# One expert load of the last step, split by rows into one transfer of 96 and four of 8

## The reference

```
def expert_block(args):
    xb, e = args
    return (jax.nn.silu(xb @ w1[e]) * (xb @ w3[e])) @ w2[e]
...
out = jnp.zeros((N + 1, D), jnp.float32).at[row_tok].add(yr.astype(jnp.float32) * row_w[:, None])
```

## Time and profile before

| | us |
|---|---|
| median of 3 runs (lowest to highest) | 675.09 (674.52 to 675.24) |
| the profiled execution, its own time | 675.29 |
| its span, from the first to the last instruction | 673.5 |
| PE busy in the span | 511.5 (76%) |
| DMA busy, mean of 16 engines, by the first queue | 89.4% |

### The profile page before, as it was taken

The page is one execution under the profiler, slowest core; times in us unless marked ns, Lnnn a source line. Parts: engine busy times, 40 slices in busy tenths (PEclk is TensorE's granted clock), DMA queues, the critical chain, the costliest instruction groups (busy, mean ns, idle before and its releaser), DMA issues.

```text
span 673.5 us, 8778 instructions
## 1 busy us (share of the span) xinstructions
PE 511.5 (76%) x3804; PEld 322.7 (48%) x3804; DVE 204.5 (30%) x378; ACT 145.5 (22%) x252; POOL 14.9 (2%) x31
## 2 busy tenths in 40 slices
PE   8999999999999997967744846774374667348475
PEld 7999998999999742422311411231141123114121
DVE  4899565588857431100000100000010000001002
ACT  5764545354635411000000000000000000000002
POOL 1200010001001000000000000000000000000001
PEclk9999999999999988997857988786797778679788
DMA  8999236908679999999999999999999999999994
GB/s 290 386 325 326 90 126 198 372 4 300 224 279 387 417 366 431 427 427 427 430 424 431 424 431 424 432 423 429 428 427 429 425 430 427 428 426 429 425 410 168
DMA packets 46041, 244.21 MB, mean 363 GB/s; under 512 B 5968, under 2 KB 15664, under 8 KB 34224
## 3 DMA queue, kind: packets, MB, share of 16 engines
q1 hardware_dynamic: 46000, 243.62, 89.4%
HBM read 242.53 MB, written 4.22 MB: 366 GB/s over the span
## 4 chain that ended last, share of the span: by engine, by line
PE 53%; DMA 44%; DVE 1%; ACT 1%; issue 0%; SPq 0%; POOL 0%; POOLq 0%
PE ps L713 16%; DMA slots_late<-in_w 13%; PE ps L1077 11%; DMA slots_own<-in_w 9%; DMA attn_data<-in_w 7%; PE ps L736 7%; PE ps L1082 6%; DMA slot_spare<-in_w 5%; DMA slot_last<-in_w 5%; DMA slot_mixed<-in_w 4%; PE ps L691 1%; DMA slots_own<-in_w_in 1%; PE ps L837 1%; PE ps L866 1%; PE ps L1187 1%; PE ps L951 1%
## 5 line engine op out<-in xcount | busy, mean ns | idle before, releaser
L1077 PE MATMUL ps<-slots_late,x_sb 128*32 128x512 f32 x320 | 88.2, 697 | 36.6 <-DMA slots_late<-in_w 14.7
L1077 PE MATMUL ps<-slot_spare,x_sb 128*32 128x512 f32 x128 | 60.8, 675 | 13.7 <-DMA attn_data<-in_w 13.7
L1077 PE MATMUL ps<-attn_data,x_sb 128*32 128x512 f32 x160 | 61.9, 701 | 10.7 <-DMA slots_own<-in_w 10.7
L1820 DVE TENSOR_TENSOR slot_extra<-ps,slot_extra 128x512 f32<-128x512 f32 x8 | 5.5, 692 | 212.2 <-ACT slot_extra L1443 212.2
L439 DVE TENSOR_TENSOR w_low<-slots_own,w_high 128x2048 fp32r<-128x2048 f32 (+1 forms) x32 | 64.7, 2021 | 16.8 <-ACT w_high L1251 16.5
L1440 ACT ACTIVATE slot_extra<-ps 128x256 f32<-128x256 f32 x8 | 3.1, 384 | 299.7 <-PE ps L1145 299.7
L1077 PE MATMUL ps<-slots_own,x_sb 128*32 128x512 f32 x240 | 56.7, 664 | 8.8 <-DMA slot_last<-in_w 3.6
L1082 PE MATMUL ps<-slots_own,slot_extra 128*32 128x512 f32 x192 | 50.1, 723 | 16.1 <-DMA slots_late<-in_w 8.0
L1082 PE MATMUL ps<-attn_data,slot_extra 128*32 128x512 f32 x112 | 46.4, 749 | 16.4 <-DMA slots_own<-in_w 16.4
L1251 ACT ACTIVATE w_high<-slots_own 128x2048 fp32r<-128x2048 f32 (+1 forms) x32 | 54.3, 1697 | 19.5 <-PE ps L736 10.8
L713 PE MATMUL ps<-h_high,w_high 128*128 128x256 f32 x224 | 55.4, 288 | 0.0
(11 more groups left out here) (262 smaller groups left out, 868.5 us busy)
## 6 DMA issues: line engine op xcount, KB each, us to landing
slots_own<-in_w SPq DMA_DIRECT2D x27, 2048.0 KB, 31.4
slots_late<-in_w SPq DMA_DIRECT2D x23, 2048.0 KB, 35.0
attn_data<-in_w SPq DMA_DIRECT2D x16, 2048.0 KB, 34.3
slot_last<-in_w SPq DMA_DIRECT2D x9, 2048.0 KB, 35.9
slots_own<-in_w_in SPq DMA_DIRECT2D x8, 2048.0 KB, 10.9
slot_spare<-in_w SPq DMA_DIRECT2D x8, 2048.0 KB, 34.7
slot_mixed<-in_w SPq DMA_DIRECT2D x7, 2048.0 KB, 34.7
slots_own<-in_w_out SPq DMA_DIRECT2D x2, 2048.0 KB, 9.7
```

Source lines behind the costliest of these rows:

```text
L1077: return pe.matmul(ps[SLOTS * e:SLOTS * e + SLOTS, 4 + matrix, :], xeT[:, k, SLOTS * e:SLOTS * e + SLOTS], w, start=(k == 0), stop=(k == K ...
L1820: dve.tensor_tensor(act_sb, ps[:, 5, :].rearrange("p (q f) -> p f q", f=FC), silu_sb.rearrange("p (f q) -> p f q", f=FC), ALU.mult).then_i ...
```

## The change

Unit 84 is no longer one transfer of 128 rows. SP issues five: rows 0 to 95 in one, which adds to `slot_in` as before, and then rows 96 to 103, 104 to 111, 112 to 119 and 120 to 127 in four, which add to a new semaphore, `split_rows_in`. PE waits for that semaphore (4 times 16) as well before the last step's first matmul. The transfer of 96 rows is spread over all sixteen DMA engines, each transfer of 8 rows over half of them. Bytes, slots and the order of the loads are the same.

```
+SPLIT_UNIT = (STEPS - 1) * MOE_CHUNKS
+SPLIT_ROWS = [(0, 96)] + [(p0, 8) for p0 in range(96, P, 8)]
...
-        extra_in = sem("extra_in")
+        extra_in, split_rows_in = sem("extra_in"), sem("split_rows_in")
...
+                elif q == SPLIT_UNIT:
+                    matrix, expert = j // SHARE, step * SHARE + j % SHARE
+                    for p0, n in SPLIT_ROWS:
+                        sp.dma_start(ring[s][p0:p0 + n].unsqueeze(1),
+                                     expert_weights[matrix][p0:p0 + n, expert:expert + 1, :]
+                                     ).then_inc(split_rows_in if p0 else slot_in[s], 16)
...
                     pe.wait_ge(slot_in[s], value)
+                    if it * MOE_CHUNKS + j == SPLIT_UNIT:
+                        pe.wait_ge(split_rows_in, 16 * (len(SPLIT_ROWS) - 1))
```

## The result

The changed kernel takes 686.46 us (median of 6 runs, 685.27 to 689.67), the kernel before 675.10 beside it (6 runs, 674.32 to 675.69): a ratio of 1.0175, interval 1.0164 to 1.0187, or 11.4 us more. The forecast was 673.9, its range ended at 679.9. The sign was the slow rival's, the size was not.

A forecast was written before the change was run, and what follows sets the result against it. The prediction took the late half of the DMA engines' last weight landing as the bound. Rows moved gave -1.22 us, all other terms 0: 675.29 to 674.07, or 673.9 us by the runs' median; range 673.2 to 679.9.

The forecast's parts named there:

- How fast the pieces run: Unit 84's small pieces writing into eight neighbouring partitions: taken at 0 us, upper end 17.1 us more for their engines.
- The pieces choke: Rival: engines writing neighbouring partitions share one's rate; share stays 1, GB/s falls; +4.4 us, 679.5 us, chance 0.38.
- Rows moved: Unit 84's rows on the DMA engines: the late half carries two fewer, so the last landing comes earlier, -1.22 us.
- the step at 0.5: DMA busy share near 0.5 before the last landing, half the engines still working; forecast to be gone.
- Four more transfers on SP: SP issuing units 85 and 86 1.7 us later, covered by a queue of some 30 us: taken as nothing.
- one more wait on PE: PE before the last step's first w1 matmul: pieces have 14.7 us before anyone waits, taken as nothing.
- PE behind the landing: PE before its last eight matmuls: still idle 0.24 us after a 1.22 us earlier landing, so nothing late.
- The wrong half: Rival: the late half of the DMA engines gets the pieces, its queue 1.22 us longer; 676.3 us, chance 0.08.
- nothing moves: Rival: eight-row transfers are dealt to all sixteen engines, each still has 8 rows; time stays 675.1 us, chance 0.07.

The follow-up runs named there:

- four by step 4: Unit 84 as four transfers of 32 rows, every fourth partition each, no small pieces, against the kernel before: 674.96 us, ratio 0.9993.
- the middle run: Unit 84 as 96 rows and four pieces of 8, each piece taking every fourth row of 96 to 127, against the kernel before: 684.39 us, ratio 1.0153.
- the run of 96 and 32: Unit 84 as one transfer of 96 rows and one of 32, no small pieces, against the kernel before: 683.91 us, ratio 1.0133.

## Why the prediction was wrong

*How fast the pieces run* is the step that failed: it was taken at 0, by the rate of large transfers, 26.75 GB/s for each engine. That row was of transfers over all 128 partitions, and it does not carry over to a block of fewer. The working asked the question only of the four small pieces. The transfer of 96 rows, with three quarters of the bytes, was counted as six plain rows for each engine; the runs show it at half rate, and 8.9 of the 11.4 us come with the four pieces joined into one transfer of 32 rows. The pieces were not free either. From the change to four by step 4 the cost goes in three steps: spreading the pieces' rows takes off 2.1 us (686.46 - 684.39), spreading the 96 rows 6.2 (684.39 - 678.24), dealing the rest without small pieces 3.3 (678.24 - 674.96). The first two are rough, since the middle run spreads over 5 us.

*The pieces choke*, the slow rival, had the mechanism in the right direction: the share stayed at 1 while GB/s fell behind 595 us, as its sign was to be. It had only the smaller of the two parts, and 4.4 us in place of 11.4; the last landing is at 673.4, not 664 to 668. The Trainium skill's rule on ports (SBUF — State Buffer, "Door 1: The DMA port swizzle") was weighed in the prediction for the pieces alone. It would not have priced the 96 rows by the count of ports: by its table rows 0 to 63 cover the 8 even ports and rows 64 to 95 lie on odd ones, all 8 by its formula, so that the transfer reaches all 16. Yet these rows ran at 203 to 229 GB/s, as 64 rows on 8 ports did. The runs agree with the rule where it counts 8 ports; what holds the 96 rows at half rate is not shown.

*Rows moved* was right in what it moves, by the shape of the end: the step at 0.5 is gone in all five runs with small pieces, while it stays in the runs of crowded blocks without them (0.51, 0.49 and 0.39 from 668.5 to 670 us in the run of 96 and 32). It was wrong in what that is worth. All five have another tail in its place, about two engines (0.12 to 0.2) that work on for 1.5 to 2 us; in the changed kernel they put the last landing 2.4 us behind the mean, where eight had put it 1.2 behind. With the crowding removed, the same deal still came out 3.1 us slower. No run gave the 1.2 us, or any part of them that could be seen.

*Four more transfers on SP*, *one more wait on PE* and *PE behind the landing* were right. The issues cost 1.4 us on SP and no gap; unit 84's 96 rows landed 15 us ahead of the matmul that waits for them, and that wait was ended by a unit behind it, attn_data; PE idled 1.45 us before its last eight matmuls, as before. *The wrong half* and *nothing moves* are out: each priced under 1.3 us, and the step at 0.5 would have stayed.

Not settled: why 96 rows in a block run at half rate, why a single crowded unit costs 3.3 us beyond its own bytes, why uncrowded pieces on half of the engines cost 3.3, and which engines are the tail. One cause could serve the two costs of 3.3, that engines thrown out of their order meet in the same places within the plain units behind, for a while; no view shows the place of a packet, so I leave it there.

## What to carry to other kernels

Before splitting a transfer, ask which partitions each transfer writes: splits by every second or fourth row ran at full rate, blocks of 64 or 96 rows and every eighth row at half. Read GB/s beside the busy share of the DMA engines, since a crowded engine is a busy one. And where a term has no row of its own in the trace, ask it of every part of the change, the largest first.

## What the runs showed of the hardware

- A transfer of 96 rows over all sixteen engines moved 203 to 229 GB/s between 600 and 607.5 us in the run of 96 and 32, one of even rows over the same engines 423 to 436. I had expected the number of engines to set the rate.
- The rate was set by the partitions written, not by the rows read: with the rows read in a block and written two apart 426 GB/s, the reverse 220.
- A crowded load slows what stands near it in the queue: one halved unit of 2 MB kept the rate at 216 to 236 GB/s for 15 us, in which 3.4 MB moved.
